# A decay matrix's rows spread over the partitions by selection matmuls instead of a trip through DRAM

## The reference

```python
def step(state, inp):
    xc, dtc, bc, cc = inp
    acum = jnp.cumsum(dtc * a, axis=1)
    seg = acum[:, :, None] - acum[:, None, :]
    decay = jnp.exp(jnp.where(causal, seg, -jnp.inf))
    cb = jnp.einsum('blgn,bsgn->blsg', cc, bc)
    xdt = xc * dtc[..., None]
    scores = cb[..., None] * decay
    y_diag = jnp.einsum('blsgr,bsgrp->blgrp', scores, xdt)
    ...
```

## Time and profile before

| | |
|---|---|
| median of three runs | 1627.19 us |
| the profiled execution, its time / its span | 1629.1 / 1627.1 us |
| PE busy | 1591.2 us (98%) |
| DVE / ACT / POOL busy | 971.6 / 824.6 / 83.4 us |
| mean granted TensorE clock | 0.996 |
| the SSD steps (scan and its preparation) | about 1141 to 1231 us |
| loads of the decay rows | 8 of 512 KB, median 5.6 us from issue to landing |

### The profile page before, as it was taken

How to read it: one execution, slowest core, us unless ns; L and a number is a source line. 1 busy time by engine, 2 the same in 40 slices (tenths; PEclk the granted TensorE clock), 3 DMA queues, 4 the chain that set the end, 5 groups by cost and what they waited for, 6 DMA issues and landing times.

```text
span 1627.1 us, 22230 instructions
## 1 busy us (share of the span) xinstructions
PE 1591.2 (98%) x8737; PEld 1367.7 (84%) x8737; DVE 971.6 (60%) x1117; ACT 824.6 (51%) x996; POOL 83.4 (5%) x86
## 2 busy tenths in 40 slices
PE   7999999999999999999989999999999999999998
PEld 7888889988888888888967888889898899888886
DVE  5564456476654464545676554469897656664454
ACT  6644443465444454445565544456787534354444
POOL 1000000010000000000120000000363000000000
PEclk9999999999999999999999999999999999999999
DMA  7665545335655555555422555556554665456552
GB/s 222 201 206 189 197 156 158 130 116 172 201 181 190 177 190 192 176 191 168 138 65 91 195 178 196 180 170 220 190 173 138 201 195 185 166 190 203 185 180 78
DMA packets 214257, 281.86 MB, mean 173 GB/s; under 512 B 9364, under 2 KB 183848, under 8 KB 214184
## 3 DMA queue, kind: packets, MB, share of 16 engines
q1 hardware_dynamic: 212904, 279.52, 52.6%
q10 hardware_dynamic: 1280, 1.32, 0.2%
HBM read 279.73 MB, written 1.08 MB: 173 GB/s over the span
## 4 chain that ended last, share of the span: by engine, by line
PE 89%; DVE 5%; ACT 4%; issue 1%; DMA 0%; POOL 0%; ACTq 0%; DVEq 0%
PE ps L1914 21%; PE ps L1916 21%; PE ps L1915 21%; PE ps L1906 6%; PE ps L1907 6%; PE ps L1908 6%; PE ps L2057 1%; DVE w_lo L1126 1%; PE ps L2028 1%; ACT scr L907 1%; ACT w_hi L630 1%; ACT scr L777 1%; DVE b_stat L1507 1%; ACT xg_hi L650 0%; PE ps L2141 0%
## 5 line engine op out<-in xcount | busy, mean ns | idle before, releaser
L1126 DVE TENSOR_TENSOR w_lo<-w_raw,w_hi 128x2048 fp32r<-128x2048 f32 x258 | 590.8, 2292 | 291.3 <-ACT w_hi L630 291.2
L630 ACT ACTIVATE w_hi<-w_raw 128x2048 fp32r<-128x2048 f32 x258 | 493.7, 1915 | 397.9 <-PE ps L1916 318.2
L1914 PE MATMUL ps<-w_hi,xg_hi 128*128 128x512 f32 x976 | 382.2, 392 | 0.6 <-DVE xg_lo L1147 0.2
L1916 PE MATMUL ps<-w_hi,xg_lo 128*128 128x512 f32 x976 | 380.1, 389 | 0.0
L1915 PE MATMUL ps<-w_lo,xg_hi 128*128 128x512 f32 x976 | 379.8, 389 | 0.0
L1914 PE MATMUL ps<-w_hi,y_hi 128*128 128x512 f32 (+1 forms) x634 | 253.5, 400 | 3.8 <-DVE y_lo L1533 3.0
L1906 PE MATMUL ps<-xg_hi,w_hi 128*128 128x256 f32 x872 | 251.3, 288 | 5.0 <-DVE xg_lo L1147 4.6
L1916 PE MATMUL ps<-w_hi,y_lo 128*128 128x512 f32 (+1 forms) x634 | 247.8, 391 | 0.0
L1907 PE MATMUL ps<-xg_lo,w_hi 128*128 128x256 f32 x872 | 247.2, 284 | 0.0
L1908 PE MATMUL ps<-xg_hi,w_lo 128*128 128x256 f32 x872 | 247.1, 283 | 0.0
L1915 PE MATMUL ps<-w_lo,y_hi 128*128 128x512 f32 (+1 forms) x634 | 246.8, 389 | 0.0
(11 more groups left out here) (326 smaller groups left out, 1194.9 us busy)
## 6 DMA issues: line engine op xcount, KB each, us to landing
w_raw<-in_ffn_w_in_dram SPq DMA_DIRECT2D x176, 512.0 KB, 4.5
w_raw<-in_ffn_w_out_dram SPq DMA_DIRECT2D x88, 512.0 KB, 4.2
w_raw<-in_w_in_dram SPq DMA_DIRECT2D x82, 512.0 KB, 4.6
w_raw<-in_a_w_in_dram SPq DMA_DIRECT2D x30, 512.0 KB, 4.6
w_raw<-in_w_gate_dram SPq DMA_DIRECT2D x22, 512.0 KB, 3.7
w_raw<-in_w_up_dram SPq DMA_DIRECT2D x22, 512.0 KB, 4.7
w_raw<-in_w_down_dram SPq DMA_DIRECT2D x22, 512.0 KB, 4.2
w_raw<-in_w_ssd_proj_dram SPq DMA_DIRECT2D x16, 512.0 KB, 4.7
```

The source lines that it names most:

```text
L630: act.activation(w_hi[:, u % RING, :], w_raw[:, u % RING, :], ACT.Copy).then_inc(w_rounded, 1)
L1126: dve.tensor_tensor(w_lo[:, s, :], w_raw[:, s, :], w_hi[:, s, :].bitcast(F32), ALU.subtract).then_inc(w_split, 1)
L1914: pe.matmul(dst, xh, hi, start=start, stop=False, skip_group_check=True)
L1916: return pe.matmul(dst, xl, hi, start=False, stop=stop, skip_group_check=True)
```

## The change

The trip through DRAM is taken out. In its place PE spreads the rows: a matmul with a stationary operand that is one column of the 32 x 32 identity, repeated 128 times (`select`), and `s_A` as the moving operand puts row h into all partitions of half a PSUM bank. `s_A` is split in a rounded high part and a low part in fp32r (`A_hi`, `A_lo`, made by DVE behind `s_A`), so there are two matmuls of 32 rows and 256 columns for each head, 64 in all. They stand in a new function `decays(j)` after unit c and before `x_turned(j)`. Banks 0 and 1 hold the four heads of a step, so `decays` waits until ACT has read the same bank for the step before. `segments` reads PSUM and moves from the end of DVE's iteration c to iteration c + 1, behind the taps and ahead of `times_dt`; ACT's `S e h 1` reads PSUM as well. The slots `s_e` shrink from eight heads to six, so that `segments` of head h waits for `scan` of head h - 5 instead of h - 7. `s_xdt` gets room for all eight steps, so that `times_dt` waits for no scan.

```diff
@@ sync, ssd()
-                def decay_rows(j):
-                    if j == 0:
-                        sp.wait_ge(rows_stored, 16)
-                    if j > 1:
-                        sp.wait_ge(act_done, act_.at(f"S e {4 * j - 5} 1"))
-                    sp.dma_start(a_slot(4 * j, 4), A_rows[4 * j:4 * j + 4, :].partition_broadcast(P)).then_inc(rows_landed[j % 2], 16)
...
-                    if c == 6:
-                        sp.wait_ge(vec_done, vec.at("S A 1"))
-                        sp.dma_start(A_rows, s_A).then_inc(rows_stored, 16)
-                    if c in A_LOAD_AT:
-                        decay_rows(A_LOAD_AT[c])
@@ scalar, exps(j)
-                                act.activation(e_slot(i)[:, 0, P:2 * P], a_slot(i)[:, 0, P:], ACT.Exp,
+                                act.activation(s_e[:, i % 6, P:2 * P], half(i % 4 // 2, i)[:, P:], ACT.Exp,
                                                bias=bias_col[:, 64 + i:65 + i]).then_inc(act_done, act_(f"S e {i} 1"))
@@ vector, dt_rows()
+                    dve.tensor_copy(select[:, :], ident[0:32, 0:32]).then_inc(vec_done, vec("S select"))
+                    dve.tensor_copy(A_hi, s_A).then_inc(vec_done, vec("S A hi"))
+                    dve.wait_ge(vec_done, vec.at("S A hi"))
+                    dve.tensor_tensor(A_lo, s_A, A_hi.bitcast(F32), ALU.subtract).then_inc(vec_done, vec("S A lo"))
@@ vector, times_dt(j)
-                    if j > 2:
-                        dve.wait_ge(pe_done, pe_.at(f"S y {4 * j - 9}"))
@@ vector, segments(j)
-                        dve.wait_ge(rows_landed[j % 2], 16 * (j // 2) + 16)
+                        dve.wait_ge(pe_done, pe_.at(f"S A {h + 1}"))
                         dve.wait_ge(vec_done, vec.at("S bias_col"))
-                        if h > 7:
-                            dve.wait_ge(pe_done, pe_.at(f"S y {h - 7}"))
+                        if h > 5:
+                            dve.wait_ge(pe_done, pe_.at(f"S y {h - 5}"))
                         rise = rise_col[:, h:h + 2].unsqueeze(3).broadcast_to([P, 2, 2, P])
-                        dve.tensor_tensor(pair02(h), a_slot(h, 2).rearrange("p h (b t) -> p h b t", b=2), rise,
+                        dve.tensor_tensor(pair02(h), ps[:, h % 4 // 2, :].rearrange("p (h b t) -> p h b t", h=2, b=2), rise,
                                           ALU.min).then_inc(vec_done, vec(f"S seg {h}"))
@@ vector, the loop over c
                     if c - 1 in CONV_AT:
                         taps(CONV_AT[c - 1], c - 1)
                     if c - 1 in STEP_AT:
+                        segments(STEP_AT[c - 1])
                         times_dt(STEP_AT[c - 1])
...
-                    if c in STEP_AT:
-                        segments(STEP_AT[c])
@@ tensor, ssd()
+                def decays(j):
+
+                    for h in range(4 * j, 4 * j + 4):
+                        if j:
+                            pe.wait_ge(act_done, act_.at(f"S e {(h - 4) | 1} 1"))
+                        else:
+                            pe.wait_ge(vec_done, vec.at("S CB 1"))
+                        pick = select[:, h:h + 1].broadcast_to([32, P])
+                        pe.matmul(half(h % 4 // 2, h), pick, A_hi, start=True, stop=False, skip_group_check=True)
+                        pe.matmul(half(h % 4 // 2, h), pick, A_lo, start=False, stop=True, skip_group_check=True).then_inc(pe_done, pe_(f"S A {h}"))
@@ tensor, the loop over c
                     if c - 2 in STEP_AT:
                         scan(STEP_AT[c - 2])
                     if c in STEP_AT:
+                        decays(STEP_AT[c])
                         x_turned(STEP_AT[c])
```

More of the change, by code:

```diff
@@ L123, in build @@
         mask = sb("mask", [P, 384])
-        band = sb("band", [P, 896])
-        window = band[:, 0:384]
+        window = sb("window", [P, 384])
         block_ones = sb("block_ones", [P, P])
@@ L135, in build @@
         gain_b = sb("gain_b", [P, 2])
-        rope = band[:, 384:896].rearrange("p (k t) -> p k t", t=T)
+        rope = sb("rope", [P, 2, T])
         small = sb("small", [P, 64])
@@ L168, in build @@
         stored = sem("stored")
-        rows_stored = sem("rows_stored")
-        rows_landed = [sem(f"rows_landed{k}") for k in range(2)]
         acc_ready = sem("acc_ready")
@@ L332, in build @@
         s_x = tiles(KB(0, 24))
-        s_xdt = tiles(KB(24, 6), 768)
+        s_xdt = tiles(KB(24, 16), 2048)
         s_cb = tiles(KB(40, 6), 384)
         s_A = KB(46, 1)[0:32]
-        s_Ab = tiles(KB(30, 8))
-        s_e, s_e2 = tiles(KB(47, 9), 384), tiles(band[:, 0:768], 384)
+        A_hi, A_lo = y_hi[0:32, 0], y_lo[0:32, 0]
+        select = sb("select", [32, 32], F32R)
+        s_e = tiles(KB(47, 9), 384)
         s_in, s_cv = mem_k, tiles(mem_v[:, :, :].rearrange("p a b -> p (a b)"))
@@ L486, in ssd @@
                 load(U["dt"], g_src(w, SSD_DT))
-                def decay_rows(j):
-                    if j == 0:
-                        sp.wait_ge(rows_stored, 16)
-                    if j > 1:
-                        sp.wait_ge(act_done, act_.at(f"S e {4 * j - 5} 1"))
-                    sp.dma_start(a_slot(4 * j, 4), A_rows[4 * j:4 * j + 4, :].partition_broadcast(P)).then_inc(rows_landed[j % 2], 16)
[L496 to L500, removed]
-                    if c == 6:
-                        sp.wait_ge(vec_done, vec.at("S A 1"))
-                        sp.dma_start(A_rows, s_A).then_inc(rows_stored, 16)
-                    if c in A_LOAD_AT:
-                        decay_rows(A_LOAD_AT[c])
+                for j in range(4):
+                    load(U["bc"] + j, g_src(w, SSD_XBC + 2048 + 256 * j))
+                for j in range(4):
+                    load(U["xs"] + j, g_src(w, SSD_XBC + 256 * j))
+                for j in range(4):
+                    load(U["xz"] + 2 * j, g_src(w, SSD_XBC + 1024 + 256 * j))
+                    load(U["xz"] + 2 * j + 1, g_src(w, 256 * j))
+                for j in range(4):
+                    load(U["z"] + j, g_src(w, 1024 + 256 * j))
                 for name, c in (("ga", SSD_GA), ("gb", SSD_GB)):
@@ L508, in ssd @@
                         load(U[name] + j, row_src(w, 512 * (j % 2), c + 512 * (j // 2)))
-                        if name == "ga" and 20 + j in A_LOAD_AT:
-                            decay_rows(A_LOAD_AT[20 + j])
                 for j in range(8):
@@ L2382, in scan @@
                         o = ps[64 * e:64 * e + 64, 2 + j % 2, t * T:t * T + T]
-                        w = e_slot(h)[:, 0]
-                        pe.matmul(o, s_xdt[:, 0, 64 * (h % 12):64 * (h % 12) + 64], w[:, 0:T], start=True, stop=False, skip_group_check=True)
-                        pe.matmul(o[:, P:], s_xdt[:, 1, 64 * (h % 12):64 * (h % 12) + 64], w[:, T:], start=False, stop=True,
+                        w = s_e[:, h % 6]
+                        pe.matmul(o, s_xdt[:, 0, 64 * h:64 * h + 64], w[:, 0:T], start=True, stop=False, skip_group_check=True)
+                        pe.matmul(o[:, P:], s_xdt[:, 1, 64 * h:64 * h + 64], w[:, T:], start=False, stop=True,
                                   skip_group_check=True).then_inc(pe_done, pe_(f"S y {h}"))
@@ L2430, in ssd @@
                         pe.wait_ge(vec_done, vec.at("S y 15"))
[L2431 removed]
+                        pe.wait_ge(act_done, act_.at("S e 29 1"))
                     if j == 4:
```

18 lines of the change are left out of this document (5 added, 13 removed).

## The result

The kernel after takes 1644.99 us, the median of four runs (1644.73 to 1646.67), beside 1627.51 us for the kernel before in the same comparison: a ratio of 1.0107, 95% interval 1.0095 to 1.0119, 17.5 us slower. The profiled execution took 1645.33 us with a span of 1643.6, which is 16.5 more than the span of before. The prediction was 1638.9 us with a range that ended at 1643: the direction was right, the size was too small by a third.

A forecast was written before the change was run, and what follows sets the result against it. PE was taken to bound the kernel (89% of the span). Matmuls 7.7 + 0.5, stalls 3.2 + 3.2 + 0.4, less 3.3 and 1.7, plus one clock fall of 1.7: +11.7 on 1627.2 us gives 1638.9 us, range 1631 to 1643.

The forecast's parts named there:

- 64 matmuls with the changes around them: On PE: 64 selection matmuls at 0.12 us, 7.7 us, plus 0.5 us for changing to and from other work.
- new stalls: PE waiting at the selection matmuls: 3.2 us at c = 13, 3.2 at c = 16, 0.4 at c = 17 and 18.
- the old stall and its slowed clock: Ahead of step 3's transposes: PE's 3.3 us wait and the 1.7 us of slow clock behind it vanish.
- slowed clock behind the new stalls: Behind PE's new waits: 0, 1 or 2 clock falls of 1.7 us each possible, one counted.
- Rival (b): On PE: weight loads not overlapped, 64 matmuls at 0.31 us, 19.8 us; +15.8 us in all, 1643.0 us; chance 0.07.
- Segments from PSUM: On DVE: 0.6 us per segment start to start, saving about 8 us, useful only where PE waits for DVE.
- rival (d): DMAs had hindered weight loads: gain at most 5.0 us, none unless matmuls cost under 0.03 us; chance 0.04, other gains included.
- No idle time ahead of the transposes of step 3: Sign in the changed profile: PE's old 3.3 us wait before these transposes is gone.
- Failed step 1: Clock term behind PE's new stalls: of 0, 1 or 2 possible falls one was taken, 1.7 us.
- rival (c): Six-slot ring binds: four stalls at c = 13, 16, 17, 18 of about 3.5 us, +19 us, 1646 us; chance 0.05.
- Failed step 3: From unit 9's end to unit 20's end 10 to 12 us longer, with nothing given back behind that.

The follow-up runs named there:

- e1: Kernel before plus the 64 selection matmuls and their three small DVE operations, results unread, rows still through DRAM: 1633.17 us, ratio 1.0023.
- e8: Kernel before with only segments moved behind the split in DVE's next iteration, rows in SBUF, eight slots, no selection matmuls: 1640.47 us, ratio 1.0067.
- e11: Kernel before with segments moved to the head of DVE's next iteration, ahead of the split, no selection matmuls: 1626.83 us, ratio 0.9995.
- e9: Kernel after with eight slots and segments at the head of DVE's next iteration, ahead of the split: 1633.94 us, ratio 1.0040.
- e3: Kernel after with eight slots for the decay tiles, so segments of head h waits for scan of head h - 7: 1638.09 us, ratio 1.0070.
- e5: Kernel after with dummy matmuls, results unread, filling PE's stalls at steps 3 and 5: 1640.34 us, ratio 1.0070.
- e2: Kernel after with the low part of A left out, 32 selection matmuls instead of 64: 1643.14 us, ratio 1.0103.
- e6: Kernel before with times_dt placed ahead of the taps in DVE's iteration: 1629.24 us, ratio 1.0006.
- e13: Kernel before with 27 matmuls, results unread, put in front of the transposes of step 3: 1627.77 us, ratio 0.9995.

## Why the prediction came out short

Its sum beside the same terms as the traces and e1 give them, in us:

| term | predicted | measured |
|---|---|---|
| 64 matmuls with the changes around them | 8.2 | 9.5 |
| new stalls | 6.8 | 5.5 |
| the old stall and its slowed clock | -5.0 | -5.0 |
| slowed clock behind the new stalls | 1.7 | 5.1 |
| lost behind the stretch | 0 | 1.8 |
| unit 9 earlier, and what is left over | 0 | -0.4 |
| together | 11.7 | 16.5 |

The first two errors cancel, which is luck.

*Matmuls: nearly right.* 0.12 us from start to start, 64 times, 7.7 us; the changes around them were 1.8 us and not 0.5. Each weight load takes 0.18 us and still they start 0.12 apart. The Trainium skill, "TensorE: Matmul & The Clock Gate", section "The mechanism", says in one place that a weight load overlaps a running matmul only where the row groups differ; all 64 use the same 32 rows, so the trace disagrees. (The same section also has loads into a background weight buffer pulled ahead, which these rows would fit and which the prediction left out.) Rival (b) is out.

*Segments from PSUM: right as a duration, of no use as a gain.* 0.67 to 0.69 us sixteen times, where from SBUF they had taken up to 1.51. That alone doesn't show that PSUM made them short: in e8 they read SBUF and took no longer, behind the split. With the segments at the head of the iteration, where other work runs beside them, the operand does tell: up to 1.51 us from SBUF (e11), none over 0.69 from PSUM (e9). In ns, min/median/max:

```profile
L1652 DVE TENSOR_TENSOR scr<-scr,ssd_small x12: 677/685/687, 1151.9 to 1232.4; 128x512 f32<-128x512 f32 x12
L1652 DVE TENSOR_TENSOR scr<-scr,ssd_small x12: 682/697/1507, 1146.5 to 1213.8; 128x512 f32<-128x512 f32 x12
L1634 DVE TENSOR_TENSOR scr<-ps,ssd_small x12: 680/691/693, 1149.3 to 1221.4; 128x512 f32<-128x512 f32 x12
```

These are e8, e11 and e9. But DVE was not full, it was waiting. The trip through DRAM cost nothing, as said: e9, where it is gone and nothing stalls, is no faster than e1, where it stays. (The bound in rival (d) is a slip: (5.0 - 0.5) / 64 is 0.07 us for each matmul, not 0.03. Nothing hangs on it.)

*No idle time ahead of the transposes of step 3: right.* They start at 1181.18, 0.21 us behind the last selection matmul.

*Stalls: right in place and mechanism, sizes mixed.* At c = 13 0.92 + 0.94 us in place of 1.9 + 1.3. At c = 16 2.25 + 0.95, which equals the 3.2 of the sum, but for another reason: with eight slots e3 has 0.94 there. My queues made the first stall too long, and I left the ring out of it. At c = 17 and 18 0.23 + 0.24 in place of 0.4.

*Failed step 1: "I take one [fall of the clock]", 1.7 us.* It was two, the second twice as long: 5.1 us. I had read the fall off one gap of 3.28 us and one of 1.90. Here a pair of gaps of 0.92 and 0.94 was followed by a fall of 1.7 us, and 2.25 + 0.95 by one of 3.4. e5 shows that this is a cost apart: with the gaps filled 3.6 us of it come back in the stretch. This is the term that was most in error.

*Failed step 2: rival (c), dismissed with "PE waits for the mark of the first exps only", 0.05.* True of PE, false of the chain. The ring holds the second segment, thereby the exponentials, thereby the *rounding*, thereby the next split and all behind it. e3 prices it at 6 us. The rival's 1646 us lies next to the 1645 measured, but by luck: it had four stalls of 3.5 us, 14 in all, where there were 5.5.

*Failed step 3: "nothing given back behind it".* The stretch sends out more than PE's delay. At its end DVE's splits and ACT's roundings are some 18 us later than before (a split at 1260.53 in place of 1242.53) and PE only 14.7, so that the lead which they had over PE is gone; the split that PE meets at 1284.60 was ready 1.5 us too late. I had followed PE to the end of unit 20 and DVE and ACT no further than c = 18.

*What lies under the three* is the loop between DVE and ACT. I costed the new order by the stalls it makes ahead of the selection matmuls. e8 shows that the order makes 11 us of loss without any selection matmul, and e11 that it hangs on which side of the split the segments stand. Behind it, the segments wait for ACT's rounding through the split, and the rounding waits for the segments through the exponentials, as e8's rows at 1166.15 and 1174.08 show. The single prices (3.8, 11, 6) add up to more than 17.5: e3 against e8 shows that the matmuls stand largely in the stalls of the late order. How the rest divides no run separates; six slots were not run with the segments ahead of the split.

## What to carry to other kernels

Where an operation moves in an engine's queue, ask first what it now stands behind, and whether that waits for somebody who waits for the operation: such a loop between two engines that each keep their order cost 11 us here, and showed in the profile as both being less busy and both waiting. Count the clock as its own term wherever new stalls come, and don't read it off the length of a gap alone (see below). And follow the engines off the critical path past the place where the critical one looks recovered.

## What the hardware showed that I had not expected

*The length of a gap did not tell whether the clock falls.* In e8 PE sat idle for 3.20 us ahead of 1207.74 and the clock stayed full; in e3 it sat idle for 0.94 us ahead of 1206.00 and the clock fell, at a price of 1.7 us. The rows of e8 and e3, with the granted clock third from the end:

```profile
1207.00:1215.00 8.00, 7.26 (x63) 7.01 (x65) 4.64 (x7) 5.30 (x13) 3.94 (x4) 1.00 0.53 193
```

```profile
1206.00:1214.00 8.00, 8.00 (x53) 7.86 (x54) 4.80 (x7) 5.04 (x12) 3.16 (x4) 0.79 0.32 98
```

In the stretch of the fourteen profiled executions each fall cost either 1.7 us (behind 0.94, 2.37, 2.61, 3.13 and 3.28 us of idle time, and behind pairs such as 0.92 + 0.94 and 2.71 + 1.18) or 3.4 (behind 4.02, 4.05 and 5.34, and behind the pair 2.25 + 0.95). In e8 gaps of 3.20, 1.02 and 0.54 us were followed by none. What else decides it I did not find.

*The stretch near 850 us*, whose code and place are the same in all kernels here, loses the clock at different places in different executions. From 846 to 854 the granted clock was 0.80 in the profiled execution of before and 0.79 after. In e3 it was 1.00 there, but 0.79 from 836 to 844, behind the gap ahead; in e2 and e6 it was full in both. The rows are those of before, and e3's two:

```profile
846.00:854.00 8.00, 5.71 (x36) 4.30 (x36) 7.31 (x13) 6.24 (x10) 0.00 (x0) 0.80 0.20 56
```

```profile
836.00:844.00 8.00, 6.62 (x42) 5.41 (x43) 5.04 (x23) 4.71 (x17) 0.00 (x0) 0.79 0.24 94
846.00:854.00 8.00, 6.54 (x58) 5.47 (x57) 7.52 (x14) 6.17 (x8) 0.00 (x0) 1.00 0.28 79
```

What it costs can be read from the time between two instructions that all fourteen kernels share, a transpose near 828 us and the last matmul of unit 9: 318.1 to 318.2 us in the six executions where the clock stayed full or fell only from 836 to 844, 319.2 to 319.4 in six where it fell from 848 on, 320.0 in two (e9 and e13) where it then stayed down longer. So the late fall costs 1.1 or 1.9 us and the early one nothing that shows. That is a part of the spread between executions of one kernel, and a reason to compare single traces by stretches and not by their spans.
